# Delta rule's inverse: two 32x32 products in place of one 64x64 in the first four levels

## The chip, the cores and the metric

The kernel runs on one core of a Trainium2 chip, in one launch. The metric is the device time of the launch in microseconds, lower is better. The median of three runs of the kernel before is 2843.4 us (2842.35 to 2843.79).

## What is computed

The reference is two layers of a mixer over 256 context tokens and 1024 latent tokens of width 1024, in float32. The first layer has an mLSTM branch and an RWKV-7 branch, the second an HGRN branch and a Hyena branch (a long convolution). The change lies in the RWKV-7 branch, a delta rule with decay, run in both directions over 8 heads of 64 by 64 state:

```python
def rwkv_scan(inputs, S):
    def step(S, xs):
        r, v, kk, w, k, a = xs
        sa = jnp.einsum('bhvk,bhk->bhv', S, -kk)
        S = S * w[:, :, None, :] + sa[..., None] * (kk * a)[:, :, None, :] + v[..., None] * k[:, :, None, :]
        return S, jnp.einsum('bhvk,bhk->bhv', S, r)
```

The kernel computes it by chunks of 64 tokens. Inside a chunk the steps depend on each other through a strictly triangular 64x64 matrix per head, and the chunk's answer needs the inverse of identity minus that matrix.

## The kernel before

**Stages.** The program is a row of stages, each with its own semaphores. Both scans are calls of `stage_rwkv_scan` (L1471), first direction 0 and then direction 1, in the first layer. Everything else (projections, mLSTM, output, the second layer) is outside of the change.

**Batches.** A scan has 20 chunks, taken two at a time: 10 batches `b` of two `lane`s. While batch b has its inverse made, the chunks of batch b - 1 are applied to the state, and the products of batch b + 1 are prepared. 8 heads are 4 pairs `j`, each with its two heads in the upper and lower 64 partitions (`part(q)` is partitions 64q to 64q + 63). So the 16 inverses of a batch are 4 `fours` (lane, jj) by 4 `quarters` (q, r), where r is the pair's parity inside jj.

**The inverse.** It is built by doubling in six levels. Level 0 is put in by VectorE (`begin_inverse`, L1859). Level n, from 1 to 5, joins neighbouring blocks of 2^n rows to blocks of 2^(n+1) rows: 4, 8, 16, 32 and at last 64. Each level is five steps over three engines:

- `turn_inverse` (L1676, PE): 4 transposes of 128x128 into the bank LOWER, and `copy_lower` (L1762, ScalarE) copies them to SBUF;
- `half_product` (L1688, PE): 16 matmuls of 64x64, strict_t times inv, into the two pair banks; bank q takes what comes from partitions of head q, so the four quarters fall on the four 64x64 tiles of the array;
- `copy_half` (L1766, ScalarE): both banks to SBUF, 128x512;
- `upper_product` (L1697, PE): 16 matmuls of 64x64, lower times half, into the same banks;
- `merge_upper` (L1865, VectorE): a predicated copy of 128x512 that takes from the product only the elements that level n adds, by a mask (`added_to_pairs(n)`, from `const_rwkv`, L558); all others keep their old value.

In the masks of levels 1 to 4 all added elements lie in the two 32x32 squares on the diagonal of the 64x64 block.

**Order of the work.** The order of PE's instructions is written out by hand in the loop over b. Between the steps of the inverse stand pieces of the neighbouring batches: `begin_chunk` (L1635), `strict_products` (L1579), `solve_chunk` (L1644), `turn_v` (L1618), `update` (L1653, L1658), `end_outputs` (L1664), `products` (L1592), `turn_keys` (L1602), `pull` (L1626). In levels 1 and 3 the order is half_product, begin_chunk, strict_products, upper_product, solve_chunk, turn_v. In levels 2 and 4 it is half_product, update, upper_product, end_outputs, products. In level 5 it is half_product, turn_keys, upper_product, pull. The first batch of a direction has no chunk to apply between its levels, the last none to prepare.

**Shapes on PE.** The stationary operand's partitions by columns give the shape of the array's tile: 64x64 for the inverse, begin_chunk, strict_products, solve_chunk, the first half of update and pull; 128x64 for the second half of update and end_outputs; 64x128 for products; the whole array for the transposes.

**DMA.** SyncE's queue loads one 512 KB window of operands per chunk into a ring of 8 (L1559). In direction 1 it also loads eight pieces of 1 MB of the next layer's modulation weight (L1561). L1782 (`copy_pulled`, ScalarE) runs once per batch, at its end, and so marks the batches in time.

Of the kernel before, what the change touches and what calls it, by code (L numbers as in the profile page):

```python
# [1470 lines left out]
def stage_rwkv_scan(p, arena, d, operands, v_dram, vT, chunk_decay, y, next_weights):  # L1471
# [7 lines left out]
    nc = p.nc  # L1479
    C, J = R_CHUNK, R_PAIRS  # L1480
# [39 lines left out]
    part = lambda q: slice(C * q, C * q + C)  # L1520
    both = [(j, q) for j in range(J) for q in range(2)]
    with ExitStack() as local:
# [4 lines left out]
        strict_t = sb("strict_t", [P, 2, 2, J, C])  # L1527
        inv = sb("inv", [P, 2, 2, J, C])
        lower = sb("lower", [P, J, 2, C])
        half = sb("half", [P, 2, J, C])  # L1530
# [16 lines left out]
        flat = lambda a: a.rearrange("p l j n -> p (l j) n")  # L1547
        fours = [(lane, jj) for lane in range(2) for jj in range(J // 2)]
        quarters = [(0, 0), (1, 1), (0, 1), (1, 0)]
        four = lambda lane, jj: lane * (J // 2) + jj  # L1550
        pair_bank = lambda which, lane, jj: bank(PAIR + which)[:, four(lane, jj) * C:(four(lane, jj) + 1) * C]
        pair_banks = p.psum[:, PAIR:PAIR + 2, 0:HALF]
        with nc.Block() as block:
# [18 lines left out]
            def _(pe):  # L1572
# [108 lines left out]
                def half_product(b, n):  # L1681
                    if n == 1:
                        pe.wait_ge(strict_read, 2 * (b + 1))
                        if b:
                            pe.wait_ge(upper_merged, TOP * b)
                    for lane, jj in fours:
                        for q, r in quarters:
                            last = nc.tensor.matmul(pair_bank(q, lane, jj)[part(r)], strict_t[part(q), b % 2, lane, 2 * jj + r, :],  # L1688
                                                    inv[part(q), b % 2, lane, 2 * jj + r, :], start=True, stop=True)
                    last.then_inc(half_ready, 1)  # L1690

                def upper_product(b, n):
                    pe.wait_ge(lower_copied, TOP * b + n)
                    pe.wait_ge(half_copied, TOP * b + n)
                    for lane, jj in fours:
                        for q, r in quarters:
                            last = nc.tensor.matmul(pair_bank(r, lane, jj)[part(q)], lower[part(r), four(lane, jj), q, :],  # L1697
                                                    half[part(r), q, four(lane, jj), :], start=True, stop=True)
                    last.then_inc(upper_ready, 1)

                for lane in range(2):
# [2 lines left out]
                turn_inverse(0, 1)  # L1704
                for b in range(B):
                    half_product(b, 1)
                    if b:
                        begin_chunk(b - 1, 0)
                    if b + 1 < B:
                        strict_products(b + 1, 0)  # L1710
                    upper_product(b, 1)
                    if b:
                        solve_chunk(b - 1, 0)
                    turn_v(b, 0)
                    turn_inverse(b, 2)
                    half_product(b, 2)
                    if b:
                        update(b - 1, 0)
                    upper_product(b, 2)
                    if b:  # L1720
                        end_outputs(b - 1, 0)
                    if b + 1 < B:
                        products(b + 1, 0)
                    turn_inverse(b, 3)
                    half_product(b, 3)
                    if b:
                        begin_chunk(b - 1, 1)
                    if b + 1 < B:
                        strict_products(b + 1, 1)
                    upper_product(b, 3)  # L1730
                    if b:
                        solve_chunk(b - 1, 1)
# [591 lines left out]
def first_layer(p, arena, hT, mix, spill, gate, x0, x1):  # L2324
# [8 lines left out]
    with ExitStack() as outer:  # L2333
        so = lambda name, shape: outer.enter_context(nc.sbuf_tensor(name, shape, F32))
        taps, mix_k = so("r_taps", [P, 2, 12]), so("r_mix_k", [P, WT])
        chunk_decay = so("r_chunk_decay", [P, 2, R_PAIRS, R_CHUNKS])
        spilled = lambda a: a.rearrange("k p t -> p k t")
        operands, bonus_dram = p.scratch["operands"], p.scratch["bonus"]
        stage_shift_taps(p, taps, mix_k)
        with ExitStack() as inner:  # L2340
            si = lambda name, shape: inner.enter_context(nc.sbuf_tensor(name, shape, F32))
            m_y, m_sums = si("m_y", [P, TILES, W]), si("m_sums", [P, TILES, M_HEADS])
            down = si("r_down", [P, 2, TOK])
            mlstm_branch(p, free, hT, m_y, m_sums, taps, down, spill)
            up = si("r_up", [P, 2, W])
            stage_gate_and_prepare(p, hT, free, w_in, m_y, m_sums, mix, spill, bonus_dram, operands, down, up, mix_k, chunk_decay)
        y = so("r_y", [P, R_CHUNKS, R_PAIRS, R_DIM])
        spare = so("next_mod_weight", [P, 2, 2 * D])
        ring = R_RING * 4 * R_PAIRS * R_CHUNK
        next_weights = lambda k: arena[:, ring + 2 * D * k:ring + 2 * D * (k + 1)] if k < KT - 2 else spare[:, k - KT + 2]  # L2350
        with ExitStack() as inner:
            vT = inner.enter_context(nc.sbuf_tensor("r_vT", [P, WT, R_CHUNK + TOK], F32))
            for d in range(2):
                stage_rwkv_scan(p, arena, d, operands, spill[3], vT, chunk_decay[:, d], y, next_weights)
        stage_finish(p, y, spilled(bonus_dram), spilled(spill[0]), mix, next_weights, free, gate[0], x0, x1, p.x1_stored, gate[1], hT)
# [1119 lines left out]
```

## Time and profile before

| | |
|---|---|
| median of three runs | 2843.4 us |
| the profiled execution, its own time | 2840.4 us |
| its span, from the first to the last instruction | 2838.5 us |
| mean granted TensorE clock | 0.941 |
| PE busy | 2573.6 us, 91% |
| DVE, ACT, POOL busy | 1277.2, 853.0, 130.1 us |
| instructions in the trace | 52909 |
| both scans of the delta rule | 1018 to 1462 us |

The profile counts PE's matrix multiplications (PE) and its weight loads (PEld) apart, and the ends of matmuls are modelled: groups that follow each other closely overlap in the rows. A float32 matmul of the code is shown as two MATMULs, each with a LDWEIGHTS ahead of it; a transpose is one. Waits, semaphores and branches are no busy time and are not counted in a row's x. "issue" as the end of an idle time means that nothing that the profile shows was waited for. The queue q8 of the DMA brings instructions, q1 the kernel's own transfers from SyncE's queue.

### The profile page before, as it was taken

What the parts mean: (1) busy time and instruction counts of PE and PEld (TensorE: products, weight loads), DVE (VectorE), ACT (ScalarE), POOL (GpSimd) and SP (SyncE); (2) the same over time, 40 slices, a digit from 0 to 9 for tenths busy, and PEclk for the clock granted to TensorE, in tenths of its full rate; (3) what the DMA queues carried; (4) which work ended last, traced back from release to release, by engine and by line L of the source; (5) the groups of instructions that cost most, each with busy time, mean ns of one, the idle gap of its engine ahead of it and who ended that gap; (6) DMA issues with size and microseconds to landing.
All of it is one profiled execution on the core that took longest, in us unless ns stands there. A gap on an engine that the chain in (4) does not pass through costs nothing. (4 is left out here: it accounts for less than half of the span.)

```text
span 2838.5 us, 52909 instructions
## 1 busy us (share of the span) xinstructions
PE 2573.6 (91%) x23480; PEld 1556.2 (55%) x23480; DVE 1277.2 (45%) x2035; ACT 853.0 (30%) x1562; POOL 130.1 (5%) x156
## 2 busy tenths in 40 slices
PE   7799999999899869979989979995977999999778
PEld 2454466666544458868864434442433658668633
DVE  3221344443277635535544522215341577777604
ACT  2111122224356625534432220012000334453401
POOL 0000000000012300000001100004000000000000
PEclk9799999999899979999999989995988999999789
DMA  6200111110246641113225320001102110000043
GB/s 258 84 30 6 37 50 51 50 51 36 105 115 149 167 141 49 34 67 137 78 74 189 112 97 30 30 1 38 57 30 90 36 31 24 24 24 2 23 163 104
DMA packets 102628, 203.82 MB, mean 72 GB/s; under 512 B 6528, under 2 KB 60928, under 8 KB 98817
## 3 DMA queue, kind: packets, MB, share of 16 engines
q1 hardware_dynamic: 89378, 150.51, 15.9%
q0 software_dynamic: 13024, 49.94, 6.1%
q8 instruction: 186, 3.05, 0.4%
q14 instruction: 40, 0.32, 0.0%
HBM read 148.01 MB, written 52.43 MB: 71 GB/s over the span
## 5 line engine op out<-in xcount | busy, mean ns | idle before, releaser
L687 PE MATMUL psum<-arena,m_fill_weight 128*128 128x512 f32 (+1 forms) x864 | 335.4, 529 | 6.1 <-DMA m_fill_weight<-in_l_w_in 6.1
L2679 PE MATMUL psum<-arena,g_weight 128*128 128x512 f32 (+1 forms) x512 | 221.8, 557 | 21.7 <-DMA g_weight<-in_l_w_in 21.1
L386 PE MATMUL psum<-arena,project_weight_y 128*128 128x512 f32 x512 | 221.6, 596 | 11.3 <-DMA project_weight_y<-in_l_w_in 11.3
L687 PEld LDWEIGHTS psum<-arena,m_fill_weight 128*128 128x128 f32 x864 | 157.1, 193 | 108.3 <-issue 91.8
L386 PEld LDWEIGHTS psum<-arena,project_weight_y 128*128 128x128 f32 x512 | 97.8, 191 | 134.7 <-issue 123.0
L386 PE MATMUL psum<-arena,project_weight_m 128*128 128x512 f32 (+3 forms) x432 | 156.5, 525 | 15.0 <-DMA project_weight_m<-in_l_w_in 15.0
L2670 PE MATMUL psum<-g_weight,arena 128*128 128x128 f32 x1152 | 153.5, 281 | 0.0
L1164 PE MATMUL psum<-gp_weight,arena 128*128 128x512 f32 x320 | 149.6, 616 | 0.0
L2061 PE MATMUL psum<-fin_weight,fin_mix 128*128 128x512 f32 x320 | 143.6, 602 | 3.0 <-POOL fin_mix L2211 3.0
L2670 PEld LDWEIGHTS psum<-g_weight,arena 128*128 128x128 f32 x1152 | 139.0, 193 | 2.8 <-issue 0.5
L386 PEld LDWEIGHTS psum<-arena,project_weight_m 128*128 128x128 f32 (+1 forms) x432 | 81.9, 190 | 90.2 <-issue 69.1
L2679 PEld LDWEIGHTS psum<-arena,g_weight 128*128 128x128 f32 x512 | 88.7, 193 | 68.9 <-issue 41.1
L2931 DVE COPY_PREDICATED g_pairs<-g_masks,psum 128x512 f32<-128x512 uint8 x128 | 93.6, 731 | 42.2 <-PE psum L2708 41.3
L1865 DVE COPY_PREDICATED r_inv<-r_masks,psum 128x512 f32<-128x512 uint32 x100 | 73.5, 735 | 70.7 <-PE psum L1697 70.7
L2061 PEld LDWEIGHTS psum<-fin_weight,fin_mix 128*128 128x128 f32 x320 | 59.8, 192 | 77.2 <-issue 73.8
L1164 PEld LDWEIGHTS psum<-gp_weight,arena 128*128 128x128 f32 x320 | 60.2, 196 | 73.3 <-issue 72.8
L1762 ACT COPY r_lower<-psum 128x512 f32<-128x512 f32 x100 | 58.3, 583 | 131.2 <-PE psum L1676 131.2
L805 ACT ACTIVATE m_fill_raw<-psum 128x512 f32<-128x512 f32 (+1 forms) x48 | 25.2, 525 | 219.2 <-PE psum L687 219.2
L2811 ACT ACTIVATE arena<-arena 128x1024 f32<-128x1024 f32 x64 | 69.3, 1082 | 37.4 <-DVE arena L2898 36.3
L1697 PE MATMUL psum<-r_half,r_lower 64*64 64x64 f32 x3200 | 72.4, 225 | 8.6 <-ACT r_half L1766 5.2
L3243 PE MATMUL psum<-y_u_tok,t_matrix 128*128 128x512 f32 x128 | 67.3, 608 | 8.7 <-DMA t_matrix<-in_transform 8.7
L2708 PEld LDWEIGHTS psum<-arena 128*32 128x32 f32 (+1 forms) x2944 | 44.2, 118 | 54.1 <-issue 33.2
(415 smaller groups left out, 4174.6 us busy)
## 6 DMA issues: line engine op xcount, KB each, us to landing
arena<-scratch_operands SPq DMA_DIRECT2D x40, 512.0 KB, 3.6
mod_weight<-in_l_mod_w SPq DMA_DIRECT2D x8, 1536.0 KB, 7.4
scratch_operands<-arena POOLq DMA_DIRECT2D x16, 640.0 KB, 8.0
scratch_operands<-arena POOLq DMA_DIRECT2D x32, 320.0 KB, 10.5
g_weight<-in_l_w_in SPq DMA_DIRECT2D x20, 512.0 KB, 3.9
m_fill_weight<-in_l_w_in SPq DMA_DIRECT2D x18, 512.0 KB, 3.8
project_weight_y<-in_l_w_in SPq DMA_DIRECT2D x4, 2048.0 KB, 7.9
scratch_spill<-m_fill_shifted POOLq DMA_DIRECT2D x12, 640.0 KB, 3.2
```

Source lines behind the costliest of these rows:

```text
L386: last = nc.tensor.matmul(p.psum[0:rows, u % 8, 0:n], lhsT, rhs, start=(k == 0), stop=(k == KT - 1))
L687: last = nc.tensor.matmul(p.psum[:, FILL + f % BANKS, 0:width], weight[:, q % PIECES, k, :], hT[:, k, at:at + width], start=(k == 0), stop ...
L1164: last = nc.tensor.matmul(p.psum[:, PROJECT + u % 2, :], hT[:, k, t * P:(t + 1) * P], weight[:, job, k, :], start=(k == 0), stop=(k == KT ...
L1697: last = nc.tensor.matmul(pair_bank(r, lane, jj)[part(q)], lower[part(r), four(lane, jj), q, :], half[part(r), q, four(lane, jj), :], star ...
L1762: nc.scalar.copy(lower[:, :, :, :].rearrange("p f q n -> p (f q) n"), narrow(bank(LOWER))).then_inc(lower_copied, 1)
L1865: nc.vector.copy_predicated(flat(inv[:, b % 2]).rearrange("p (f r) n -> p r f n", r=2), added_to_pairs(n), pair_banks.rearrange("p r (f n) ...
L2061: last = nc.tensor.matmul(p.psum[:, OUT + 2 * (t % 2) + n, :], mixed[:, t % SLOTS, k, :], weight[:, k, n * BANK:(n + 1) * BANK], start=(k ...
L2670: last = nc.tensor.matmul(bank[:, (t - part[0]) * P:(t - part[0] + 1) * P], hT[:, kk, t * P:(t + 1) * P], w[:, kk, :], start=(kk == 0), st ...
L2679: last = nc.tensor.matmul(bank[:, 0:width], w[:, kk, :], hT[:, kk, first:first + width], start=(kk == 0), stop=(kk == KT - 1))
L2811: nc.scalar.activation(out, out, ACT.Exp).then_inc(sig["exps_ready"], 1)
L2931: nc.vector.copy_predicated(pairs[:, w % 2, 4 * g:4 * g + 4, :], mask(units[w][1], n), chunked(p.psum[:, SCORES + m % RING, :])).then_inc( ...
L3243: last = nc.tensor.matmul(p.psum[:, 4 * part + 2 * (t // 4) + n, :], left, right[:, t, :], start=(t % 4 == 0), stop=(t % 4 == 3))
```

## The change

`half_product` and `upper_product` loop over `squares(n)`, the list of (first, size) on the diagonal. For n = 5 this is the whole block, as before. For n = 1 to 4 it is (0, 32) and (32, 32): each matmul takes the 32 partitions from `first` of its half as contraction, and 32 columns of both operands from the same `first`, and writes 32 partitions by 32 columns. The number of matmuls of such a step goes from 16 to 32. What lies outside the two squares in the pair banks is no longer written in these levels. Copies, merges, masks and all waits are the same.

```diff
+        whole = [(0, C)]
+        squares = lambda n: whole if 2 << n > 32 else [(0, 32), (32, 32)]
+        inner = lambda q, first, size: slice(C * q + first, C * q + first + size)
...
                     for lane, jj in fours:
-                        for q, r in quarters:
-                            last = nc.tensor.matmul(pair_bank(q, lane, jj)[part(r)], strict_t[part(q), b % 2, lane, 2 * jj + r, :],
-                                                    inv[part(q), b % 2, lane, 2 * jj + r, :], start=True, stop=True)
+                        for first, size in squares(n):
+                            cols = slice(first, first + size)
+                            for q, r in quarters:
+                                last = nc.tensor.matmul(pair_bank(q, lane, jj)[inner(r, first, size), cols],
+                                                        strict_t[inner(q, first, size), b % 2, lane, 2 * jj + r, cols],
+                                                        inv[inner(q, first, size), b % 2, lane, 2 * jj + r, cols], start=True, stop=True)
                     last.then_inc(half_ready, 1)
...
                     for lane, jj in fours:
-                        for q, r in quarters:
-                            last = nc.tensor.matmul(pair_bank(r, lane, jj)[part(q)], lower[part(r), four(lane, jj), q, :],
-                                                    half[part(r), q, four(lane, jj), :], start=True, stop=True)
+                        for first, size in squares(n):
+                            cols = slice(first, first + size)
+                            for q, r in quarters:
+                                last = nc.tensor.matmul(pair_bank(r, lane, jj)[inner(q, first, size), cols],
+                                                        lower[inner(r, first, size), four(lane, jj), q, cols],
+                                                        half[inner(r, first, size), q, four(lane, jj), cols], start=True, stop=True)
                     last.then_inc(upper_ready, 1)
```

## Rows read from the trace of the kernel before

**Rows 1.** The page: busy time, granted clock by slices, the instruction queue.

```profile
PE 2573.6 (91%) x23480; PEld 1556.2 (55%) x23480; DVE 1277.2 (45%) x2035; ACT 853.0 (30%) x1562; POOL 130.1 (5%) x156
PEclk9799999999899979999999989995988999999789
q8 instruction: 186, 3.05, 0.4%
```

**Rows 2.** Windows, both scans: length, busy (x) by engine, clock, DMA share, GB/s.

```profile
1018.00:1462.00 444.00, 411.44 (x12007) 363.05 (x12009) 221.64 (x425) 202.90 (x435) 11.01 (x18) 0.97 0.21 71
```

**Rows 3.** Timeline of PE, levels 3 and 4 of one batch: start, length in us.

```profile
1116.97 0.69 PE L1688 MATMUL psum<-r_inv,r_strict_t 64*64 64x64 f32 x32
1117.48 0.63 PE L1635 MATMUL psum<-r_state,arena 64*64 64x64 f32 x16
...
1121.13 0.63 PE L1653 MATMUL psum<-r_state,arena 64*64 64x64 f32 x16
1121.69 0.69 PE L1658 MATMUL psum<-r_uv,r_k_tok 128*64 128x64 f32 x16
```

**Rows 4.** Windows, one undisturbed batch of direction 0.

```profile
1169.52:1189.82 20.30, 20.30 (x613) 18.12 (x614) 11.13 (x21) 10.56 (x23) 0.61 (x1) 1.00 0.02 4
```

**Rows 5.** DMA, both scans: packets, MB, share of 16 engines; loads and their KB.

```profile
q8 instruction: 95, 1.56, 1.5%
...
arena<-scratch_operands SPq DMA_DIRECT2D x32, 512.0 KB, 3.5
arena<-in_l_mod_w SPq DMA_DIRECT2D x6, 1024.0 KB, 6.8
next_mod_weight<-in_l_mod_w SPq DMA_DIRECT2D x2, 1024.0 KB, 6.4
```

**Rows 6.** DMA, the batch of rows 4: GB/s in 40 slices, queue.

```profile
GB/s 0 0 0 0 0 0 0 32 0 0 0 0 0 0 0 32 16 0 0 0 0 0 0 32 0 0 0 0 0 0 0 32 0 0 0 0 0 0 0 0
...
q8 instruction: 4, 0.07, 1.5%
```

**Rows 7.** Timeline of PE, direction 1, behind a 1 MB load.

```profile
1287.39 0.50 PE L1658 MATMUL psum<-r_uv,r_k_tok 128*64 128x64 f32 x9 [1.44 <-issue]
```

**Rows 8.** DMA from 1284 to 1292 us, 40 slices of 0.2 us.

```profile
GB/s 451 246 82 82 205 41 0 0 0 0 0 0 0 0 0 0 0 0 0 0 0 0 0 82 0 0 0 0 0 0 164 143 205 246 348 266 369 492 430 389
...
q8 instruction: 2, 0.03, 1.7%
```

**Rows 9.** Timeline of PE, direction 0, no load near.

```profile
1109.25 0.28 PE L1579 MATMUL psum<-arena 64*64 64x64 f32 x4
1109.85 0.51 PE L1579 MATMUL psum<-arena 64*64 64x64 f32 x11 [0.32 <-issue]
```

**Rows 10.** DMA from 1106 to 1114 us, 40 slices of 0.2 us.

```profile
GB/s 0 0 0 0 82 0 0 0 0 0 0 0 0 0 0 0 0 0 0 0 0 0 0 0 0 82 0 0 0 0 0 0 0 0 0 0 0 0 0 0
```

**Rows 11.** DMA from 1193 to 1201 us, 40 slices of 0.2 us.

```profile
GB/s 0 0 0 0 0 0 82 0 0 0 0 0 0 0 0 0 0 0 0 0 0 0 0 82 0 0 0 0 0 0 0 0 0 0 0 0 0 0 0 0
```

**Rows 12.** Line L1782, each direction: duration ns, first and last start us.

```profile
L1782 ACT COPY r_pulled<-psum x10: 586/586/586, 1046.7 to 1229.2; 128x512 f32<-128x512 f32 x10
...
L1782 ACT COPY r_pulled<-psum x10: 586/586/586, 1271.6 to 1462.5; 128x512 f32<-128x512 f32 x10
```

**Rows 13.** DMA from 1278 to 1285 us, 40 slices of 0.175 us.

```profile
GB/s 0 0 0 0 0 94 0 0 0 0 0 0 211 140 94 140 374 398 398 421 445 468 515 187 468 281 421 562 140 609 94 609 234 562 421 374 47 94 140 187
```

**Rows 14.** Timeline of PE, level 5.

```profile
1104.47 0.69 PE L1688 MATMUL psum<-r_inv,r_strict_t 64*64 64x64 f32 x32
1105.10 1.09 PE L1602 MATMUL psum<-consts,arena 128*128 128x128 f32 x8
```

**Rows 15.** Timeline of PE and a line's durations, tiles 32 wide in the HGRN branch.

```profile
2301.37 0.46 PE L2708 MATMUL psum<-arena 128*32 128x32 f32 x32
...
L2708 PE MATMUL psum<-arena x2944: 196/196/369, 2237.4 to 2665.8; 128*32 128x32 f32 x188, 128*64 128x64 f32 x9
```

**Rows 16.** Windows, the end of direction 0 and the beginning of direction 1.

```profile
1205.00:1235.00 30.00, 26.11 (x776) 22.64 (x770) 10.75 (x20) 14.84 (x32) 0.00 (x0) 1.00 0.01 3
...
1241.40:1254.90 13.50, 9.19 (x116) 7.96 (x116) 5.08 (x10) 1.17 (x2) 1.17 (x2) 0.50 0.80 311
```

**Rows 17.** Timeline of PE, first batch of direction 0.

```profile
1031.69 1.13 PE L1688 MATMUL psum<-r_inv,r_strict_t 64*64 64x64 f32 x32
```

## The prediction

> **What bounds the kernel now.** I read the page first: TensorE (PE) is busy for 91% of the span, nearly everywhere at the full granted clock, so time is won or lost on PE's instruction stream [rows 1]. The change touches the two scans of the delta rule alone, from 1018 to 1462 us. There PE is busy 411 of 444 us, DVE 222 and ACT 203 [rows 2]: the copies and merges that follow each level have room, PE has none.
>
> Then the timeline of PE over two levels [rows 3]. Each group begins before the modelled end of the one before, so no wait stands between them. A group of the inverse is x32: the 16 matmuls of the code are two MATMULs each, and each of these has a LDWEIGHTS of its own. In an undisturbed batch of two chunks PE issues 613 MATMULs and 614 LDWEIGHTS in 20.3 us, at clock 1.00 [rows 4].
>
> Last, where do instructions come from? PE's come by DMA. The instruction queue (q8) brings 16 KB a packet, 186 in the run [rows 1] and 95 in this stretch [rows 5], so 24,016 instructions shown by 95 packets, 253 a packet: with the waits that are not counted, 256. One undisturbed batch has its packets 8 slices of 0.51 us apart, 4.1 us [rows 6]. Two places tell how far ahead they come. At 1287.39 PE resumes in the middle of L1658 after 1.44 us without work, released by nothing ("issue") [rows 7]. The packet had started at 1285.0; the next one starts at 1288.6, 1.3 us after PE resumed, with the DMA queues empty in between [rows 8]. The same at 1109.85 in L1579 [rows 9]: packets at 1106.8 and 1111.0 [rows 10]. So one block is fetched while one is executed, and the next fetch starts only when PE enters the block just fetched. **The fetch cycle** is then 2.4 + 1.3 = 3.7 us at the first place and 2.9 + 1.3 = 4.2 us at the second; the shortest distance of two fetches that I found is 17 slices of 0.2 us, 3.4 us [rows 11]. I take 3.8, between the three and nearest to the places where PE did run dry, and keep 3.4 and 4.2. A batch of 1227 instructions is 4.85 blocks, 18.4 us of fetching in 20.3 us: hidden now, by a tenth.
>
> **The change, part by part.** Nothing is removed but columns and rows of work. For levels 1 to 4 each of the 16 matmuls of half_product and upper_product becomes two of 32x32: 32 in the code, 64 MATMULs and 64 LDWEIGHTS in the trace. Per batch that is 8 groups by 64 instructions more, 512, exactly 2.0 blocks; level 5, copies (L1762, L1766) and merges (L1865) keep their shapes. No DMA is issued by the code in addition, no wait is added.
>
> *Fetching.* 4.85 + 2.0 = 6.85 blocks a batch, by 3.8 us: 26.0 us against 20.3. Sixteen batches are full; the last one of each direction prepares no next batch (136 instructions fewer) and has 6.3 blocks. Together 122 blocks, 464 us. Before, these 18 take 182.5 us in the first direction and 190.9 in the second, from the first to the last copy of L1782 [rows 12], 373.4 in all. **+91 us** (+42 at 3.4, +140 at 4.2).
>
> *The first batch of each direction* has the levels without the chunk's part between them, and waits for data there, which covers some of its fetching: by its share of the new instructions +3 us each, **+6** (2 to 8).
>
> *Loads beside fetches.* In the second direction eight loads of 1 MB follow loads of 512 KB [rows 5]; a fetch behind them is late (one starts at 1278.9, the next at 1285.0 [rows 8, 13] instead of some 4.1 us later). Now that costs 190.9 - 182.5 = 8.4 us, since part of the lateness falls into slack. Without slack all of it counts, up to 2 us by eight; the 464 us have none of it. **+10** (5 to 16).
>
> *Executing.* This is the smaller term, and it lies under the fetches. Switching the array's shape costs: L1688 starts 0.51 us before L1635, of its own shape [rows 3], and 0.63 us before L1602, of another [rows 14]; the group behind a switch takes 0.69 us (L1658) where one without takes 0.63 (L1653) [rows 3]. So 0.15 to 0.18 us a switch. The new 32x32 groups of levels 1 and 3 stand between 64x64 ones: three switches more each; in levels 2 and 4 only half_product meets one (L1653): one more each. Eight a batch, 1.2 us. The pace of 32x32 tiles is not in the trace. The nearest rows are the 32-wide tiles of L2708: x32 in 0.46 us, of which 0.20 is one matmul's own length, 8.4 ns a MATMUL [rows 15]; the 64x64 groups go by (0.69 - 0.22)/31 = 15.2 ns [rows 3]. Bounds: 4.2 ns if eight tiles overlap as four do there, 15.2 ns if the tile's width does not matter. I take 8.4: 64 MATMULs span 0.53 us from first to last start, against 0.47: +0.06 us by eight groups, +0.5 us. A batch would execute in 20.3 + 1.2 + 0.5 = 22.0 us: less than the 26.0 us of fetching, so it costs nothing; without this cover it would cost 1.7 us a batch, about +30 us in all. At 15.2 ns it would be 25.4 us, still covered.
>
> Here a page speaks. The rows show blocks of 16 KB, one ahead [rows 5, 7 to 10], and stalls behind them. The Trainium skill, "Runtime: NRT & Kernel Launch", section "Instruction fetch mechanics", gives the same blocks of 256 instructions and says that crossing one is "mostly hidden". By that the sum would be only the execution's +30 us; it is the first rival.
>
> **Sum:** 91 + 6 + 10 = +107 us on the profiled execution's 2840.4 us (span 2838.5), 2947 us. The median of the runs, 2843.4, is 3.0 higher: **2950 us**. Low ends: 42 + 2 + 5 = +49, 2892; high ends: 140 + 8 + 16 = +164, 3007.
>
> **Rivals.**
> *Fetches stay hidden, switches count.* If more than one block can come ahead once PE asks faster, what stays is +30 us: 2873 (2850 to 2885 by the bounds of the pace). For it: fetches have seldom stopped PE so far. Against: the next fetch waited for PE at both places where PE was dry, when it had most reason to run ahead [rows 8, 10].
> *The clock falls.* PE would idle a quarter of the time in this stage. If the granted clock went to 0.50, 1.2 GHz, as between 1241 and 1255 us [rows 16], groups would take 1.6 times as long: L1688's x32 takes 1.13 us at 0.50 [rows 17] and 0.69 at 1.00 [rows 3]. The 22.0 us of a batch would be 36, above the fetches, and 20 batches some 310 us longer: near 3155. Against: from 1205 to 1235 us PE has pauses, is busy 26 of 30 us, and the clock stays at 1.00 [rows 16].
> *Faster.* If 32x32 and 64x64 tiles do not need a switch between them, since both are cuts of one array, and eight tiles overlap at 4.2 ns, a group's last start comes 0.19 us sooner: 160 groups, -30 us, 2813. It decides only if a block's fetch takes less than 18.8 us / 6.85 = 2.7 us; the trace has none below 3.4 [rows 11]. The Trainium skill, "TensorEngine Tiling (Array Packing)", "Theoretical Speedup", counts both dimensions as a gain of tiling; the rows price a group by its instructions as much as by its columns.
> *It does not do what it says.* If the time of a stage with doubled instructions stayed as it is, within 6 us: nothing in the rows makes them free.
>
> **How the numbers follow.** Fetch-bound 0.83; fetches hidden 0.08; clock 0.03; faster 0.03; nothing 0.03. The time is the fetch-bound one. The range takes its case from 2885 to 3005, nearly all of it, which leaves some 0.2 outside. A measurement of this kernel can tell 0.2%, 5.7 us, from no change. Faster 0.03, same 0.03, slower 0.94.
>
> **What would show it.** q8 brings about 135 packets between the scans' first and last instruction instead of 95, 226 in the run instead of 186, and 3.8 us apart in undisturbed batches. L1782's copies lie about 26 us apart. PE's idle time with "issue" as its end grows to over 80 us, in pieces of 0.5 to 1.5 us in the middle of groups of any line; DVE and ACT are as busy as before and idle longer. L1688 and L1697 show x5760 each: 20 batches by (4 x 64 + 32). Between stalls L1688 starts 0.6 us or more before L1635 where it was 0.51. It would be wrong if packets came under 3.4 us apart, or if the batches took some 22 us with no idle "issue": then the first rival holds.

## The result, and the profile after

The changed kernel is slower: 2974.3 us, median of six runs (2969.9 to 2985.0), against 2842.8 us for six of the kernel before (2833.4 to 2843.8). The ratio is 1.0477, 95% interval 1.0453 to 1.0501, +131 us at the medians. The forecast was 2950 us with a range of 2885 to 3005: its direction was right, its size 24 us short. The profiled execution took 2981.2 us, 6.9 above its median; the profiles below set it beside that of the kernel before, 2840.4 us.

The page of the changed kernel, beside [rows 1]:

```profile
PE 2646.4 (89%) x28600; PEld 1610.2 (54%) x28600; DVE 1278.3 (43%) x2035; ACT 856.8 (29%) x1562; POOL 130.1 (4%) x156
...
q8 instruction: 226, 3.70, 0.5%
```

5120 MATMULs and 5120 LDWEIGHTS more, and 40 packets of instructions more, as forecast (226). DVE and ACT have not one instruction more and are as busy as before. What stands behind the two scans takes the same time: from the last of the copies that end a batch (at 1603.4 us here, at 1462.5 before) to the end of the span it is 1375.9 us (2979.3 less 1603.4) against 1376.0.

The windows of the batches 2 to 10 of each direction, from the first to the last copy that ends a batch, first the changed kernel and then the kernel before (columns as in [rows 2]):

```profile
1056.75:1302.18 245.43, 209.86 (x7748) 181.01 (x7748) 95.56 (x179) 96.82 (x207) 4.91 (x8) 0.95 0.10 30
1349.75:1603.41 253.66, 213.42 (x7748) 185.22 (x7748) 101.18 (x197) 90.47 (x190) 4.91 (x8) 0.93 0.18 62
```

```profile
1046.65:1229.16 182.51, 180.69 (x5444) 160.64 (x5444) 95.11 (x179) 95.01 (x208) 4.92 (x8) 1.00 0.12 39
1271.63:1462.50 190.87, 183.26 (x5444) 162.15 (x5444) 100.73 (x197) 88.34 (x189) 4.92 (x8) 1.00 0.23 81
```

Lengths first: 499.1 us against 373.4, +125.7 us for 18 batches, 27.3 us each in direction 0 and 28.2 in direction 1. Length less busy time is what PE idled: 75.8 us against 9.4, +66.4. The last column but two is the granted clock, which was 1.00 and is 0.95 and 0.93. The rest of the +140.8 us between the two spans stands in the first batches of the two directions, and 4.5 us of it ahead of the scans, where the change is not.

Who ended the idle time? The waits of the changed kernel, PE alone, both scans (microseconds in total, times, longest). Its lines are numbered anew: half_product is L1693, upper_product L1705, strict_products L1582, products L1595, turn_v L1621, solve_chunk L1647, update L1656 and L1661, end_outputs L1667, turn_inverse L1679.

```profile
PE psum L1705 <- issue: 33.7, 29, 1.9
PE psum L1693 <- issue: 19.9, 26, 1.9
PE psum L1582 <- DMA arena<-scratch_operands: 10.4, 2, 6.4
PE psum L1621 <- issue: 5.4, 4, 3.1
PE psum L1647 <- issue: 5.2, 4, 1.7
```

With the smaller rows "issue" has 76.9 us in 80 pieces, spread over nine lines, against 6.6 us in 9 pieces in the kernel before. The one DMA wait is the old one at the beginning of a direction. The timeline of PE shows two of them in level 2 (or 4) of a batch, each in the middle of a group:

```profile
1208.54 0.60 PE L1679 MATMUL psum<-consts,r_inv 128*128 128x128 f32 x4
1209.07 0.35 PE L1693 MATMUL psum<-r_inv,r_strict_t 32*32 32x32 f32 x30
1210.15 0.46 PE L1693 MATMUL psum<-r_inv,r_strict_t 32*32 32x32 f32 x34 [0.74 <-issue]
1210.54 0.68 PE L1656 MATMUL psum<-r_state,arena 64*64 64x64 f32 x16
1211.15 0.69 PE L1661 MATMUL psum<-r_uv,r_k_tok 128*64 128x64 f32 x16
1211.76 0.72 PE L1705 MATMUL psum<-r_half,r_lower 32*32 32x32 f32 x61
1213.83 0.25 PE L1705 MATMUL psum<-r_half,r_lower 32*32 32x32 f32 x3 [1.35 <-issue]
```

From 1210.15 to 1213.83 PE executes 34 + 16 + 16 + 61 = 127 MATMULs and about as many LDWEIGHTS: with the waits, which are not counted, one block of 256. It takes 3.7 us, of which 1.35 are waiting. The DMA of 1206 to 1218 us, 40 slices of 0.3 us, shows the packets that it waits for:

```profile
GB/s 109 14 0 0 0 55 0 0 0 0 0 0 0 0 0 0 0 55 0 0 0 0 0 0 0 0 0 0 0 0 55 0 137 164 300 396 369 300 41 27
```

They start at 1207.5, 1211.1 and 1215.0, 3.6 and 3.9 us apart, with nothing else on the queues. PE resumes at 1210.15 and the next packet starts 1.1 us later; it resumes at 1213.83 and the next starts 1.3 us later (a slice is 0.3 us). This is the pattern of [rows 8] and [rows 10], now in block after block.

### The profile page after: what moved, and what is told of

It is laid out like the page before. It is cut to its first block and busy times, and to the rows that moved or that the text cites. A ratio compares the mean times of both kernels' runs of the same rounds, so it can differ in the third digit from the quotient of the medians.

```text
span 2979.3 us, 63149 instructions
## 1 busy us (share of the span) xinstructions
PE 2646.4 (89%) x28600; PEld 1610.2 (54%) x28600; DVE 1278.3 (43%) x2035; ACT 856.8 (29%) x1562; POOL 130.1 (4%) x156
## 5 line engine op out<-in xcount | busy, mean ns | idle before, releaser
L1705 PE MATMUL psum<-r_half,r_lower 32*32 32x32 f32 (+1 forms) x5760 | 79.8, 204 | 37.7 <-issue 33.7
L1693 PE MATMUL psum<-r_inv,r_strict_t 32*32 32x32 f32 (+1 forms) x5760 | 82.2, 209 | 20.0 <-issue 19.9
L1705 PEld LDWEIGHTS psum<-r_half,r_lower 32*32 32x32 f32 (+1 forms) x5760 | 64.6, 110 | 50.7 <-issue 43.7
L1693 PEld LDWEIGHTS psum<-r_inv,r_strict_t 32*32 32x32 f32 (+1 forms) x5760 | 66.9, 114 | 43.0 <-issue 42.8
```

Of the source, the lines that this page charges most:

```text
L1693: last = nc.tensor.matmul(pair_bank(q, lane, jj)[inner(r, first, size), cols], strict_t[inner(q, first, size), b % 2, lane, 2 * jj + r, cols],
L1705: last = nc.tensor.matmul(pair_bank(r, lane, jj)[inner(q, first, size), cols], lower[inner(r, first, size), four(lane, jj), q, cols], half ...
```

## The experiments

All ratios are to the kernel before, run on the same chip. Times of different experiments are not all of one chip: the changed kernel itself had 2974.3 us on one and 2982.6 us on another. The levers are the number of instructions, the switches of shape and the length of the loads.

**As many instructions, no 32x32 tile.** Each 64x64 matmul of levels 1 to 4 is issued twice, with half of the columns moving.

```diff
+        columns_of = lambda n: [slice(0, 32), slice(32, 64)] if n <= 4 else [slice(0, C)]
...
-                        for q, r in quarters:
-                            last = nc.tensor.matmul(pair_bank(q, lane, jj)[part(r)], strict_t[part(q), b % 2, lane, 2 * jj + r, :],
-                                                    inv[part(q), b % 2, lane, 2 * jj + r, :], start=True, stop=True)
+                        for cols in columns_of(n):
+                            for q, r in quarters:
+                                last = nc.tensor.matmul(pair_bank(q, lane, jj)[part(r), cols], strict_t[part(q), b % 2, lane, 2 * jj + r, :],
+                                                        inv[part(q), b % 2, lane, 2 * jj + r, cols], start=True, stop=True)
```

> The kernel before, with each 64x64 matmul of levels 1 to 4 cut in two by its columns: the same 64x64 stationary operand twice, 32 columns moving each time. It issues exactly as many instructions as the changed kernel (6.85 blocks a batch), but no tile is 32x32 and no shape of the array changes. Theory (instruction fetch): as slow as the changed kernel up to its switches, batches of 26 to 27 us, time 2945 to 2975, q8 with 226 packets. Rival (switches of shape, pace of small tiles, or the clock dips that come with them): batches near 20.5 us, time 2840 to 2860.

Measured 2978.5 us, ratio 1.0488 (1.0462 to 1.0513), 226 packets: the changed kernel's time, without its tiles and switches, and 3.5 us above the range of the theory. But the rival was priced too low. The timeline has its groups at

```profile
1106.99 1.14 PE L1690 MATMUL psum<-r_inv,r_strict_t 64*64 64x32 f32 x64
1107.95 0.66 PE L1636 MATMUL psum<-r_state,arena 64*64 64x64 f32 x16
1108.44 0.63 PE L1580 MATMUL psum<-arena 64*64 64x64 f32 x16
1108.92 1.14 PE L1700 MATMUL psum<-r_half,r_lower 64*64 64x32 f32 x64
```

and 0.96 us from one group's start to the next instead of 0.51. A group of twice as many MATMULs with half the columns takes twice as long, so this kernel executes 8 times 0.45 = 3.6 us more a batch than before, 72 us in 20. That alone would give some 2916; 63 us more are left for the fetches. The better comparison is with the changed kernel: two kernels whose executing differs by 2 us a batch and whose instructions are equal in number come out 4 us apart. What this one executes longer it waits less: "issue" has 42.3 us in 64 pieces here, against 76.9 in 80. In direction 0 its nine intervals take 240.5 us, and that at clock 1.00:

```profile
1053.18:1293.69 240.51, 222.34 (x7748) 198.84 (x7748) 96.64 (x179) 96.96 (x208) 4.94 (x8) 1.00 0.10 31
```

**Half of the added instructions.** upper_product is taken back to whole blocks:

```diff
-                        for first, size in squares(n):
-                            cols = slice(first, first + size)
-                            for q, r in quarters:
-                                last = nc.tensor.matmul(pair_bank(r, lane, jj)[inner(q, first, size), cols],
-                                                        lower[inner(r, first, size), four(lane, jj), q, cols],
-                                                        half[inner(r, first, size), q, four(lane, jj), cols], start=True, stop=True)
+                        for q, r in quarters:
+                            last = nc.tensor.matmul(pair_bank(r, lane, jj)[part(q)], lower[part(r), four(lane, jj), q, :],
+                                                    half[part(r), q, four(lane, jj), :], start=True, stop=True)
```

> The changed kernel, but upper_product is the one of before (whole 64x64 blocks); only half_product goes by squares. 5.85 blocks a batch. Theory (fetch): 5.85 blocks by 3.8 to 4.0 us are 22.2 to 23.4 us a batch, barely above the 21.1 us of executing, so about a third of the loss: 2880 to 2905, q8 with 206 packets. Rival (executing): half_product has two of the three extra switches in levels 1 and 3 and all in 2 and 4, so well over half of the loss stays: 2910 to 2930.

Measured 2898.7 us, ratio 1.0213 (1.0184 to 1.0242), 206 packets. +55 us of the +131: inside the range that the theory of the fetches gave, and below that of the rival.

**All switches, no added instruction.**

```diff
-        squares = lambda n: whole if 2 << n > 32 else [(0, 32), (32, 32)]
+        squares = lambda n: whole if 2 << n > 32 else [(0, 32)]
...
+            if 1 <= n <= 4:
+                added = added & (s < 32) & (t < 32)
             cols += [added]
```

> The changed kernel with only the first of the two 32x32 squares multiplied and merged in levels 1 to 4 (the second square's part of the inverse is left out; its masks are empty there). Per batch the number of instructions is that of the kernel before (4.85 blocks), and every switch between 64x64 and 32x32 stays. Theory (fetch): no stalls are added; a group is 0.2 us shorter and the switches cost 0.8 us a batch, so 19.5 to 20.3 us a batch, 2828 to 2845. Rival (switches or clock): 2860 or more.

Measured 2835.9 us, ratio 0.9980 (0.9963 to 0.9998): no slower, if anything 0.2% faster. The timeline has every switch of the changed kernel; a group is one of 32x32 tiles, x32, in 0.45 us:

```profile
1065.67 0.45 PE L1695 MATMUL psum<-r_inv,r_strict_t 32*32 32x32 f32 x32
1066.05 0.68 PE L1640 MATMUL psum<-r_state,arena 64*64 64x64 f32 x16
1066.57 0.63 PE L1584 MATMUL psum<-arena 64*64 64x64 f32 x16
1067.13 0.45 PE L1707 MATMUL psum<-r_half,r_lower 32*32 32x32 f32 x32
1067.51 0.68 PE L1649 MATMUL psum<-r_rest,r_inv 64*64 64x64 f32 x16
```

```profile
L1793 ACT COPY r_pulled<-psum x10: 585/585/586, 1045.9 to 1222.2; 128x512 f32<-128x512 f32 x10
```

Its nine intervals of direction 0 take 176.4 us against 182.5, as the theory expected. So the switches are not what costs the 131 us.

**More instructions still.** On top of the change, level 5 is cut by columns as in the first experiment (half_product is shown; upper_product has the same edit).

```diff
+        columns_of = lambda first, size: [slice(0, 32), slice(32, 64)] if size == C else [slice(first, first + size)]
...
-                            cols = slice(first, first + size)
-                            for q, r in quarters:
+                            weights = slice(first, first + size)
+                            for cols, (q, r) in [(c, quarter) for c in columns_of(first, size) for quarter in quarters]:
```

> The changed kernel with, in addition, level 5's 64x64 matmuls cut in two by their columns (64x64 stationary, 32 moving): 128 instructions more a batch, 7.35 blocks, no new switch. Theory (fetch): 0.5 block by 20 batches by 3.8 to 4.0 us, +35 to +40 us on the changed kernel: 3005 to 3020, q8 with 236 packets. Rival (executing): at most 0.1 us a group, +4 us: 2975 to 2980.

Measured 3002.1 us, ratio 1.0575 (1.0542 to 1.0608), 236 packets: 3 us below the range of the theory. That is +28 us on the changed kernel's 2974.3, which ran on another chip, so 35 to 40 is not excluded; the rival's 4 is. This rival was also priced too low: by the first experiment's 0.45 us a group, executing alone would add 0.9 us a batch, 18 us in 20. So this run speaks for the fetches less clearly than it was meant to. By packets the four kernels stand so: 186, 206, 226, 236 packets, and 2843.5 (before), 2898.7, 2974.3, 3002.1 us. Each of the second twenty costs 3.8 us, of the first 2.8, of the last ten 2.8.

**The loads beside the fetches.** The 1 MB loads of direction 1 are cut in four and issued a level of the inverse apart, in the kernel before and in the changed one:

```diff
-                        sp.dma_start(next_weights(s - SLOTS), p.dram["l1_mod_w"].rearrange("(p k) n -> p k n", k=KT)[:, s - SLOTS, 0:2 * D]
-                                     ).then_inc(next_loaded, 16)
+                        source = p.dram["l1_mod_w"].rearrange("(p k) n -> p k n", k=KT)
+                        for piece in range(4):
+                            if piece:
+                                sp.wait_ge(half_ready, TOP * ((s - SLOTS) // 2 + 1) + (2, 4)[(s - SLOTS) % 2] + piece)
+                            at_piece = slice(piece * D // 2, (piece + 1) * D // 2)
+                            sp.dma_start(next_weights(s - SLOTS)[:, at_piece], source[:, s - SLOTS, at_piece]).then_inc(next_loaded, 16)
```

> The kernel before, with each 1 MB load of direction 1 cut into four of 256 KB, issued at four levels of the inverse instead of at once behind the window's 512 KB. Theory (an instruction packet that starts behind a long load is late and stops PE): the stalls of direction 1 shrink, its batches go from a mean of 21.2 us to 20.4 to 20.6, 5 to 8 us in all: 2835 to 2839. Rival (those stalls are no matter of the load's length): 2842 to 2845.

> The changed kernel with the same cut of the 1 MB loads. Theory (without slack the whole lateness counts): direction 1's batches go from a mean of 28.2 us to direction 0's 27.3, 8 us in all: 2963 to 2969. Rival (the loads cost nothing beyond the fetch cycle): within 2 us of the changed kernel's 2974.

Both missed the range of the theory. In the kernel before: 2841.0 us, ratio 0.9992 (0.9980 to 1.0005), no difference that can be told from none. Its stalls did not go: the timeline of direction 1 has one of 1.74 us,

```profile
1301.73 0.63 PE L1701 MATMUL psum<-r_half,r_lower 64*64 64x64 f32 x27 [1.74 <-issue]
```

where the longest of direction 1 in the kernel before is 1.44. The loads are shorter and four times as many.

In the changed kernel: 2972.5 us, ratio 1.0449 (1.0434 to 1.0464). By its time it fits the rival, 1.8 us below the changed kernel's median, but the two are of different chips, and by the ratios (1.0477, 1.0453 to 1.0501) it is some 8 us faster, with intervals that overlap. Its profile speaks for the theory: direction 1 takes 251.2 us and direction 0 250.7, nearly the same, where direction 1 is longer by 8.2 us in the changed kernel and by 11.7 in its second profile (last experiment). But direction 0, which the edit leaves alone, is itself 5 us longer than in the changed kernel's profile. That a fetch is late beside a load stands by [rows 8, 13]. That the load's length is what counts was not found in the kernel before, and is open in the changed one.

**One switch less.** end_outputs goes ahead of upper_product in levels 2 and 4, so that the two 128x64 steps of a chunk stand together.

```diff
                         update(b - 1, 0)
-                    upper_product(b, 2)
-                    if b:
                         end_outputs(b - 1, 0)
+                    upper_product(b, 2)
```

> The kernel before, with end_outputs set ahead of upper_product in levels 2 and 4: both 128x64 steps of a chunk then stand together, and one switch of the array's shape goes, two in a batch. Theory of executing (a switch costs 0.15 us, and PE is what the kernel before waits for): 18 batches by 0.3 us, 5 us: 2836 to 2840. Rival (a switch is free, or the saved time is lost to the next wait or to fetching): within 2 us of before, or slower.

> The kernel before with both edits, the loads cut in four and end_outputs ahead of upper_product. If both gains hold and are apart from each other: 10 to 13 us, 2830 to 2834. If the faster PE runs into the fetch cycle (4.85 blocks by 3.9 us are 18.9 us of some 20.0), a part of it is lost: 2834 to 2838.

> The kernel before with end_outputs ahead of upper_product, once more: if the 12 us below before were the edit's, 2828 to 2836 again; if the edit is worth only the 5 us of its switches and the rest was the chip's, 2836 to 2841.

Measured 2831.1 us, ratio 0.9960 (0.9946 to 0.9973), 5 us below the expected range, and again, on another chip, 2834.7 us, 0.9966 (0.9953 to 0.9979): 10 to 12 us, 0.3 to 0.4%, faster than the kernel before, and the fastest version here that computes the whole result. The timeline shows L1664 start 0.52 us behind L1658, with no switch between them:

```profile
1068.21 0.69 PE L1658 MATMUL psum<-r_uv,r_k_tok 128*64 128x64 f32 x16
1068.73 0.64 PE L1664 MATMUL psum<-r_uv,r_prod 128*64 128x64 f32 x16
1069.30 0.69 PE L1697 MATMUL psum<-r_half,r_lower 64*64 64x64 f32 x32
```

An undisturbed batch takes 20.02 us instead of the 20.30 of [rows 4]:

```profile
1043.02:1063.04 20.02, 20.02 (x613) 17.98 (x614) 11.31 (x21) 10.56 (x24) 0.62 (x1) 1.00 0.18 57
```

That would be 5 us in 18 batches, but the profile does not have them where they should be. The nine intervals of direction 0 take 182.2 us (181.0 in the second run) against 182.5, since some of these batches wait for instructions and are longer; those of direction 1 take 186.5 (187.2) against 190.9. So most of the gain stands in direction 1, and why was not found. With the loads cut too it is 2838.0 us, 0.9979 (0.9969 to 0.9989), at the upper end of the second expectation: the gain is smaller, not larger.

**The same edit in the changed kernel.**

> The changed kernel with end_outputs ahead of upper_product in levels 2 and 4, the edit that takes 0.28 us of executing from each batch of the kernel before. Theory (the changed kernel waits for instructions, whose number is the same): executing is hidden, so within 3 us of the changed kernel on the same chip. Rival (it waits for executing): the same 5 to 12 us as in the kernel before.

> The changed kernel as it is, for the comparison on this chip: 2970 to 2980.

The changed kernel had 2982.6 us here, ratio 1.0483 (1.0464 to 1.0501), above the expected 2970 to 2980. With the edit it had 2969.2 us, 1.0439 (1.0420 to 1.0458): 13 us less on the same chip where the theory allowed 3, and 5 us less than the changed kernel's 2974.3 on another chip. So executing is not hidden in the changed kernel as I had held, at least not all of it. The windows of the batches, with the edit and then without:

```profile
1052.20:1291.50 239.30, 204.29 (x7748) 177.15 (x7748) 96.42 (x179) 96.67 (x208) 4.91 (x8) 0.96 0.10 31
1339.00:1593.70 254.70, 211.38 (x7748) 183.88 (x7748) 101.86 (x197) 90.97 (x190) 4.92 (x8) 0.93 0.17 62
```

```profile
1052.10:1302.50 250.40, 214.47 (x7748) 185.22 (x7748) 95.60 (x179) 97.21 (x208) 4.92 (x8) 0.93 0.10 29
1347.50:1609.60 262.10, 216.21 (x7748) 187.41 (x7748) 100.86 (x197) 90.80 (x189) 4.92 (x8) 0.92 0.18 60
```

Of the 18.5 us between them (512.5 less 494.0), 15.0 are PE's busy time and only 3.5 its idle time. The clock is higher with the edit: the time at half clock, twice what is missing to 1.00, is 55 us against 77. Five of the 15 us would be the switches. What the rest is was not found: the changed kernel alone, with no edit, differs by 13.4 us between its two profiles (499.1 and 512.5 us).

## Why the prediction came out as it did

*What bounds, and the fetch cycle.* Right. PE's instructions come in blocks of 256, one ahead, and the next is asked for when PE enters the last fetched one: at the four stalls read here and in [rows 7 to 10] the next packet starts 1.1 to 1.3 us after PE resumes. Two readings were slightly off and change nothing: the parts of the cycle at the second place are 3.0 and 1.2 us, with the same sum, and the shortest distance of two packets in the scans of the kernel before is 3.3 us. The changed kernel waits so 80 times, and the number of instructions alone, by whatever edit, sets most of the time (first three experiments).

*Fetching, +91 us, and loads, +10.* The fetches' term was mis-sized: 18 batches grew by 125.7 us where the two terms together had 101. The loads' term held: direction 1 takes 8.2 us more than direction 0. Twice direction 0 is 490.9 us, so the fetches made +117.5 us and not +91. What failed is the step "6.85 blocks a batch, by 3.8 us". The number of blocks was right (61 packets in each window), and so was the cycle: the median distance of two packets is 3.86 us in direction 0 and 3.94 in direction 1. But the step takes every block at the fetch's length, and some blocks execute longer than a fetch takes; what they exceed it by is not given back by the others. So the mean is 4.0 us a block in direction 0. A block that holds level 5 and L1595 is such a one, at full clock, with no load near it:

```profile
1242.40:1247.40 5.00, 5.00 (x126) 4.36 (x125) 2.92 (x5) 2.59 (x5) 0.00 (x0) 1.00 0.01 3
```

Its 251 instructions execute in 5.0 us without a pause, since 12 transposes of the whole array (L1679, L1605) and 16 MATMULs of 64x128 (L1595) are among them, and the packets asked for at its beginning and its end start 5.0 us apart. Of the 120 distances of packets in the two windows, the 89 with fewer than 12 transposes, at full clock and beside no 1 MB load, have a mean of 3.9 us; the 8 with 12 or more have 4.4, and the 5 beside a 1 MB load 5.0.

*Executing, covered.* Its price was right and its cover was not whole. From half_product to turn_v a level 1 or 3 takes longer by 0.49 us. Before, from L1688 to L1618, it is 2.57 us:

```profile
1116.97 0.69 PE L1688 MATMUL psum<-r_inv,r_strict_t 64*64 64x64 f32 x32
...
1119.54 0.66 PE L1618 MATMUL psum<-consts,r_vT 128*128 128x128 f32 x4
```

After, from L1693 to L1621, it is

```profile
1204.98 0.75 PE L1693 MATMUL psum<-r_inv,r_strict_t 32*32 32x32 f32 x64
1205.67 0.68 PE L1638 MATMUL psum<-r_state,arena 64*64 64x64 f32 x16
...
1206.74 0.75 PE L1705 MATMUL psum<-r_half,r_lower 32*32 32x32 f32 x64
1207.43 0.68 PE L1647 MATMUL psum<-r_rest,r_inv 64*64 64x64 f32 x16
1208.04 0.66 PE L1621 MATMUL psum<-consts,r_vT 128*128 128x128 f32 x4
```

3.06 us. Levels 2 and 4 take some 0.3 us more. That is 1.5 to 1.6 us a batch, forecast 1.7. The pace of the 32x32 tiles is (0.75 - 0.19)/63 = 8.9 ns, 8.4 taken. In the blocks that are not bound by a fetch this price is paid; the forecast had it at nothing.

*The clock.* It was a rival of 0.03 with the price of a fall for the whole stage. It does not fall for the stage; it falls in pieces. The window of one:

```profile
1214.80:1218.20 3.40, 3.40 (x44) 2.85 (x48) 1.50 (x4) 0.83 (x2) 0.00 (x0) 0.50 0.50 159
```

It comes behind the stalls of 0.74 and 1.35 us shown above; in the batches of the kernel before the clock is 1.00 throughout. By the clocks of the windows some 60 of the 499 us are at 1.2 GHz. What they cost can only be estimated, since a block that executes slower waits less for the next one. Of the 120 distances of packets, 18 have 1 us or more of half clock in their block; against the others of their kind (few transposes, 12 or more, beside a 1 MB load) they are longer by 6 us in all. And direction 0 of the first experiment has clock 1.00, and still takes 240.5 us where 61.1 blocks by 3.8 us are 232. So the clock is a smaller part of what the forecast was short by. That direction also had 33 stalls, up to 1.5 us long, with PE busy 92% of the time, and the clock stayed: that the stalls bring the clock down is likely, and not shown. No run took the clock alone away.

*First batches.* +3 us each were forecast; the profiles have 5 to 6.

*Rivals.* "Fetches stay hidden" and "faster" fell with the 80 stalls; the one's price, 30 us for executing, was about right. That its range held is in part luck: its upper bound of 2885 leaves out the 15.2 ns for a MATMUL, by which the forecast's own 25.4 us a batch would have given some 2935. The clock's rival says that PE would idle a quarter of the time; its own 22.0 of 26.0 us are 15%, which is what the profile has (75.8 of 499.1 us). The Trainium skill's "mostly hidden", from "Runtime: NRT & Kernel Launch", "Instruction fetch mechanics", holds for the kernel before (9.4 us of idle time in 373) and not for this one; its blocks, one fetched while one is executed, are what the traces read here show.

## What to carry to other kernels

Count instructions as a resource of their own: a stretch of small matmuls, each with its weight load, can be bound by the arrival of instructions while PE (busy 85% here), copies and DMA all have time. The sign is idle time ended by "issue" in the middle of groups, and instruction packets at a constant distance; here a block of 256 needs 3.7 to 4 us, some 15 ns an instruction, and a MATMUL with its LDWEIGHTS 30 ns. The groups of 64x64 execute one in 15.2 ns and those of 32x32 in 8.9, so they run ahead of their instructions, and only the slower instructions between them make up for it. Cutting work into more and smaller matmuls can then cost time even where each gets faster, as here. Steps of one array shape should stand together: moving one pair of steps gave 0.3 to 0.4%.

## What the hardware showed beside this

- A float32 MATMUL of a 64x64 tile with 32 columns moving took as long as one with 64: a group of 64 of them is 1.14 us, (1.14 - 0.22)/63 = 14.6 ns each, against 15.2 ns with 64 columns. With 32x32 tiles, and also 32 columns moving, it is 8.9 ns. So the pace went with the size of the stationary operand and not with the columns that move.
- A switch of the array's shape costs some 0.15 us: an undisturbed batch of the kernel before takes 20.30 us, and 20.02 with two switches less.
- In the changed kernel, with a stall every few microseconds, the granted clock fell to 0.50 in pieces, though PE was busy 84 to 86% of these windows (209.86 of 245.43 us, 213.42 of 253.66) and no stall of direction 0 was over 1.9 us.
- The part of the program ahead of the scans is the same in all these kernels, and the first transpose of the inverse starts between 1016.0 and 1023.8 us in the profiles read: a difference of under some 8 us between two single profiles can stand outside of the change.
